# Layer 0's index stage and both stick-breaking stages in a new order: which instruction goes ahead of which on five engines

## What is computed

```python
# stick-breaking branch, per head and block of 128 queries
z = q @ k.T * dh ** -0.5
log_1m = where(mask, log_sigmoid(-z), 0)
csum = cumsum(log_1m)
a = where(mask, exp(log_sigmoid(z) + csum[-1:] - csum), 0)
y_a = a @ v
# sparse branch: scores that choose 128 keys for each query
s_idx = relu(einsum('bqhd,bkd->bqhk', iq, ixk) * IDX_DIM ** -0.5)
score = einsum('bqh,bqhk->bqk', iw * IDX_HEADS ** -0.5, s_idx)
_, sel = top_k(score, topk)
# latent branch
k_b = rope(rms_norm(concat(k_nope, k_pe)), cos, sin)
```

## Time and profile before

| | us |
|---|---|
| median of 3 runs (1336.82 to 1338.01) | 1337.74 |
| the profiled execution's own time | 1335.52 |
| its span in the trace | 1333.8 |
| PE busy | 1268.9 (95%) |
| DVE busy | 773.2 (58%) |
| ACT busy | 609.0 (46%) |

### The profile page before, as it was taken

One profiled execution on the slowest core, in us unless ns is written; L12 is line 12 of the kernel. 1 busy time (PEld: TensorE's weight loads), 2 busy tenths in 40 slices (PEclk: granted clock), 3 DMA queues, 4 the chain that ended last, 5 costly groups with the idle time before them and its releaser, 6 DMA issues.

```text
span 1333.8 us, 17870 instructions
## 1 busy us (share of the span) xinstructions
PE 1268.9 (95%) x6530; PEld 959.7 (72%) x6538; DVE 773.2 (58%) x1572; ACT 609.0 (46%) x1131; POOL 194.4 (15%) x316
## 2 busy tenths in 40 slices
PE   5898999999899999999999999999999999999998
PEld 5556666555578888888888876655556888888887
DVE  5878777888634344434456477878864424434442
ACT  4346566666653232233244365676666322323330
POOL 1372111133420000000000021113343000000000
PEclk9999999999999999999999999999999999999999
DMA  7244012201322333333332312220123322333321
GB/s 219 86 137 100 31 61 48 63 1 40 91 93 95 95 95 108 104 97 103 92 84 78 96 32 64 48 64 1 34 78 112 96 95 64 125 95 95 95 95 63
DMA packets 118568, 109.15 MB, mean 82 GB/s; under 512 B 34512, under 2 KB 101200, under 8 KB 118480
## 3 DMA queue, kind: packets, MB, share of 16 engines
q1 hardware_dynamic: 118480, 107.99, 27.1%
HBM read 100.64 MB, written 7.34 MB: 81 GB/s over the span
## 4 chain that ended last, share of the span: by engine, by line
PE 76%; DVE 9%; ACT 8%; issue 5%; SPq 1%; DMA 1%; POOL 0%; ACTq 0%; DVEq 0%
PE bank L837 20%; PE bank L839 20%; PE bank L838 20%; PE bank L983 3%; PE bank L1151 2%; PE bank L1194 2%; PE bank L1178 2%; PE bank L792 1%; DVE w_lo L729 1%; PE bank L1007 1%; ACT w_hi L723 1%; DVE probs L2043 1%; ACT soft L1482 1%; PE bank L1024 1%; ACT soft L1484 1%
## 5 line engine op out<-in xcount | busy, mean ns | idle before, releaser
L837 PE MATMUL bank<-h_hi,w_hi 128*128 128x512 f32 (+1 forms) x928 | 361.5, 390 | 4.0 <-DVE w_lo L729 2.2
L839 PE MATMUL bank<-h_hi,w_lo 128*128 128x512 f32 (+1 forms) x928 | 353.5, 381 | 0.0
L838 PE MATMUL bank<-h_lo,w_hi 128*128 128x512 f32 (+1 forms) x928 | 353.2, 381 | 0.0
L729 DVE TENSOR_TENSOR w_lo<-raw,w_hi 128x2048 fp32r<-128x2048 f32 (+2 forms) x98 | 189.1, 1931 | 119.4 <-ACT w_hi L723 119.3
L837 PEld LDWEIGHTS bank<-h_hi,w_hi 128*128 128x128 f32 x928 | 176.4, 190 | 50.5 <-issue 12.1
L723 ACT CAST w_hi<-raw 128x2048 fp32r<-128x2048 f32 (+2 forms) x100 | 159.1, 1593 | 112.5 <-PE bank L839 110.1
L839 PEld LDWEIGHTS bank<-h_hi,w_lo 128*128 128x128 f32 x928 | 176.2, 190 | 33.4
L838 PEld LDWEIGHTS bank<-h_lo,w_hi 128*128 128x128 f32 x928 | 176.4, 190 | 32.7 <-issue 1.9
L1666 ACT ACTIVATE gate<-bank,gains 128x512 f32<-128x512 f32 x48 | 33.0, 688 | 166.1 <-PE bank L839 166.1
L2228 POOL TENSOR_SCALAR probs<-probs,stat 128x128 f32<-128x128 f32 (+3 forms) x128 | 76.0, 594 | 147.3 <-DVE stat L1998 139.9
L837 PE MATMUL bank<-br_hi,w_hi 128*128 128x512 f32 x192 | 74.7, 389 | 0.0
(11 more groups left out here) (239 smaller groups left out, 2228.1 us busy)
## 6 DMA issues: line engine op xcount, KB each, us to landing
raw<-in_w_in SPq DMA_DIRECT2D x56, 1024.0 KB, 5.2
raw<-in_w_branch SPq DMA_DIRECT2D x12, 1024.0 KB, 5.2
raw<-in_w_out SPq DMA_DIRECT2D x8, 1024.0 KB, 5.0
bias<-bias_dram SPq DMA_DIRECT2D x16, 256.0 KB, 3.1
bias<-bias_dram SPq DMA_DIRECT2D x16, 192.0 KB, 2.6
x_sb<-in_x SPq DMA_DIRECT2D x4, 512.0 KB, 4.5
bias_dram<-bias_out SPq DMA_DIRECT2D x8, 256.0 KB, 2.9
raw<-in_w_in SPq DMA_DIRECT2D x4, 512.0 KB, 4.6
```

The costliest lines, as they stand in the source:

```text
L729: e.tensor_tensor(w_lo[:, s % RING, a:b], raw[:, s % RAW, a:b], w_hi[:, s % RING, a:b].bitcast(F32), ALU.subtract).then_inc(*lo_signal(nam ...
L837: pe.matmul(out_ap, lh, rh, start=start and i == 0, stop=False)
L838: pe.matmul(out_ap, lh, rl, start=False, stop=False)
L839: mm = pe.matmul(out_ap, ll, rh, start=False, stop=stop and i == n - 1)
```

## The change

Seven edits in the order of the code; nothing is computed otherwise, and no instruction is added but for a pair that is issued one by one.

1. DVE: the comparisons of G 3 go ahead of the three small ix_k operations, and those of G 7 ahead of the remainder of slab 2.
2. ACT and DVE: slab 5 is rounded ahead of the first index relu, not behind the fourth; its remainder is taken ahead of score 0, not score 4.
3. ACT: the sine goes between relu 15 and 16, the second table load between relu 19 and 20; both stood ahead of the copies of sa_v.
4. DVE: `first_rope` is split in two, ahead of scores 16 and 20.
5. ACT and POOL, both layers: for i mod 4 = 1 `stick_probs(i - 1)` and its masks go ahead of `softplus(i)` and its masks.
6. ACT, both layers: for i mod 4 = 2 `stick_probs(i - 1)` and `rounded(i)` alternate by head. In step 15 the norm of ds_q2 goes ahead of `softplus(15)`.
7. PE, both layers: `prep_q(0)` goes ahead of `pv_of(14)`.

```diff
@@ PE
+                    if i == STEPS:
+                        prep_q(0)
                     if i >= 2:
                         pv_of(i - 2)
                     if NORM_AT.get(i) in EARLY:
                         norm_tile(NORM_AT[i])
                     fill(i, "a")
-                    if i == STEPS:
-                        prep_q(0)
@@ ACT, index stage
+                    hi(5)
                     index_relus(0)
-                    hi(5)
                     index_relus(1)
                     index_relus(2)
                     index_relus(3)
+                    e.wait_ge(*angle_step.at("angle"))
+                    e.activation(ang[64:P, :], turns[64:P, :], ACT.Sin).then_inc(*cos_done.tick("sin"))
                     index_relus(4)
+                    e.preload_act_table_set("natural_log_exp_and_others")
                     index_relus(5)
...
-                if layer.l == 0:
-                    e.wait_ge(*angle_step.at("angle"))
-                    e.activation(ang[64:P, :], turns[64:P, :], ACT.Sin).then_inc(*cos_done.tick("sin"))
-                    e.preload_act_table_set("natural_log_exp_and_others")
@@ ACT, stick-breaking
+                    if i % ST == 1:
+                        stick_probs(i - 1)
+                    if i == STEPS - 1:
+                        norm_scale(NORM_AT[i])
                     softplus(i)
                     split_part(i, 0)
-                    early = i % 2 == 0 and i % ST
+                    early = i % ST == 2
                     if early:
-                        rounded(i)
+                        for head in range(2):
+                            stick_probs(i - 1, head)
+                            rounded(i, head)
                     tile_done(DONE.get((i, "a")))
-                    if NORM_AT.get(i) in EARLY:
+                    if NORM_AT.get(i) in EARLY and i < STEPS - 1:
                         norm_scale(NORM_AT[i])
-                    if i:
+                    if i and i % ST in (0, 3):
                         stick_probs(i - 1)
@@ DVE
+                if layer.l == 0:
+                    reaches(e, 3, 4)
                 e.tensor_copy(ix_k_low[top, :], dbank("k_pe")[top, :]).then_inc(*dve_evac.tick("ix_k hi"))
...
-                    reaches(e, 3, 7)
+                    reaches(e, 4, 7)
                     ix_q_parts(0)
+                    reaches(e, 7, 8)
                     split_lo(e, SLABS[2])
-                    reaches(e, 7, 11)
+                    reaches(e, 8, 11)
...
-                    if layer.l == 0 and u == 4:
+                    if layer.l == 0 and u == 0:
                         split_lo(e, SLABS[5])
+                    if layer.l == 0 and u == 16:
+                        first_rope_products()
+                    if layer.l == 0 and u == 20:
+                        first_rope_sums()
```

More of the change, by code:

```diff
@@ L1484, in softplus, with rounded @@
                         e.activation(v, v, ACT.Ln, bias=1.0).then_inc(*stick_exp.tick("ln", u))
-                def rounded(p):
+                def rounded(p, head=None):
                     for u, o, pair, kt, w in stick_units(p):
+                        if head not in (None, o):
+                            continue
                         e.wait_ge(*sp_masked.at(u))
@@ L1492, in rounded, with stick_probs @@
                         e.copy(sp_hi[:, o, SOFF[kt]:SOFF[kt] + w], soft[u % 4][:, 0:w]).then_inc(*sp_rounded.tick(u))
-                def stick_probs(p):
+                def stick_probs(p, head=None):
                     for u, o, pair, kt, w in stick_units(p):
+                        if head not in (None, o):
+                            continue
                         e.wait_ge(*stick_sum.at(u))
@@ L1767, in ix_q_parts, with first_rope_products, first_rope_sums @@
                                     ).then_inc(*dve_evac.tick(f"ix_q{j}"))
+                def first_rope_products():
+                    rows, low_rows = slice(64, 96), slice(96, P)
+                    e.wait_ge(*cos_done.at("sin"))
+                    e.wait_ge(*gains_in.at("b", DEPTH - 1, 2))
+                    e.tensor_scalar(cos_sin[64:P, :], ang[64:P, :], sign[64:P, :], None, ALU.mult).then_inc(*setup_dve.tick("cs"))
+                    e.wait_ge(*setup_dve.at("cs"))
+                    e.scalar_tensor_tensor(turns[rows, :], k_rope[low_rows, :], gain[low_rows, 4:5], cos_sin[low_rows, :],
+                                           ALU.mult, ALU.mult).then_inc(*dve_evac.tick("kr low"))
+                    e.scalar_tensor_tensor(k_rope[rows, :], k_rope[rows, :], gain[rows, 4:5], cos_sin[rows, :],
+                                           ALU.mult, ALU.mult).then_inc(*dve_evac.tick("kr0"))
+                def first_rope_sums():
+                    rows, low_rows = slice(64, 96), slice(96, P)
+                    e.wait_ge(*dve_evac.at("kr0"))
+                    e.tensor_tensor(k_rope[low_rows, :], k_rope[rows, :], turns[rows, :], ALU.add).then_inc(*dve_evac.tick("kr1"))
+                    e.tensor_tensor(k_rope[rows, :], k_rope[rows, :], turns[rows, :], ALU.add).then_inc(*dve_evac.tick("kr"))
                 e.wait_ge(*dense.at("k_pe"))
                 top, low = slice(0, IDX_DIM), slice(IDX_DIM, 2 * IDX_DIM)
+                if layer.l == 0:
+                    reaches(e, 3, 4)
                 e.tensor_copy(ix_k_low[top, :], dbank("k_pe")[top, :]).then_inc(*dve_evac.tick("ix_k hi"))
@@ L1936, in stick_out @@
                     e.tensor_copy(y[:, pair, :], bank[Y][:, :]).then_inc(*y_out["stick"].tick(pair))
[L1938 to L1947, removed]
-                                           ALU.mult, ALU.mult).then_inc(*dve_evac.tick("kr0"))
-                    e.wait_ge(*dve_evac.at("kr0"))
-                    e.tensor_tensor(k_rope[low_rows, :], k_rope[rows, :], turns[rows, :], ALU.add).then_inc(*dve_evac.tick("kr1"))
-                    e.tensor_tensor(k_rope[rows, :], k_rope[rows, :], turns[rows, :], ALU.add).then_inc(*dve_evac.tick("kr"))
-                if layer.l == 0:
-                    first_rope()
                 for i in range(STEPS):
@@ L2192, in _, with mask_probs @@
                                     channel_multiplier=1).then_inc(*score_masked.tick(t))
+                def mask_probs(p):
+                    for u, o, pair, kt, w in stick_units(p):
+                        d = stick_a[:, o, 0:P]
+                        e.wait_ge(*stick_prob.at(u))
+                        e.affine_select(out=d, in_=d, pattern=[[1, P]], compare_op=ALU.is_gt, fill=0.0, base=0,
+                                        channel_multiplier=-1).then_inc(*prob_masked.tick(u))
                 for i in range(STEPS + 1):
+                    if i % ST == 1:
+                        mask_probs(i - 1)
                     if i < STEPS:
@@ L2199, in _ @@
                                             channel_multiplier=-1).then_inc(*sp_masked.tick(u))
-                    if i:
-                        for u, o, pair, kt, w in stick_units(i - 1):
-                            d = stick_a[:, o, 0:P]
-                            e.wait_ge(*stick_prob.at(u))
-                            e.affine_select(out=d, in_=d, pattern=[[1, P]], compare_op=ALU.is_gt, fill=0.0, base=0,
-                                            channel_multiplier=-1).then_inc(*prob_masked.tick(u))
+                    if i and i % ST != 1:
+                        mask_probs(i - 1)
                     if i == 2:
```

## The result

The changed kernel took 1324.34 us in the median of 4 executions (1322.54 to 1326.56), the kernel before 1337.80 beside it: a ratio of 0.9902, 95% interval 0.9882 to 0.9921. That is 13.5 us faster, and 13.4 against the 1337.74 from which the prediction started; 1326.3 was predicted. The profiled execution took 1326.56, with a span of 1324.8, so it is the longest of the four, and 8.96 us under the profiled execution of before.

The account below looks back on a forecast made before the run. PE was busy 1268.9 of 1333.8 us, so only its waits could be saved, unless its clock moved. Terms 4.3 + 3.0 + 1.6 + 1.1 + 1.4 = 11.4 us off the 1337.74 median gave 1326.3, range 1322.3 to 1331.3.

Parts of the forecast that it names:

- Bias table, 4.3 us: Bias table, edit 1: PE through at 46.6 instead of 50.9, 4.3 us saved, clock included.
- Index scores, 3.0 us: Index stage, edits 2 to 4: of 4.4 us of waits for relu and sa_v, 1.4 paid back, 3.0 saved.
- With 2.3 score 0 is done at 100.0: Index scores: if slab 5's remainder takes 2.3 us on DVE, score 0 ends at 100.0 and relu 3 at 100.4.
- score 4 at 103.4: Index scores: score 4 at 103.4 gives relu 7 at 103.9, wanted at 104.3, so the 2.0 us wait goes.
- Clock at step 0, 1.6 us: Step 0 of layer 0: fills follow shorter pauses of 0.6 and 1.1 us and run at full clock, 1.6 us saved.
- Clock at ix_q0, 1.5 us: ix_q0 behind G 3: with a pause of 0.4 us the clock stays up, another 1.5 us saved.
- the first rival: Clock falls again behind new pauses, taking back 1.2 us at ix_q0 and 1.6 at step 0: 1329.1; chance 0.19.
- Stick-breaking, 1.1 and 1.4 us: Stick-breaking stages, edits 5 and 6: key sums first saves 1.1 us in layer 0 and 1.4 in layer 1.
- two of the rivals: Softplus held behind key sums: stick-breaking gains nothing, 1331, chance 0.12; or the kernel gets slower, 1341, chance 0.02.
- prep_q, 0 us: End of each stick-breaking stage, edits 6 and 7: prep_q(0) ahead of pv(14) saves 0 us, bounds -0.3 and +1.6 a layer.
- waits for its norm product: prep_q(0) overwrites the bank of ds_q2, so it waits for that norm product, 248.77 to 249.52 before the change.
- my two clock terms: Full clock kept at ix_q0, 1.5 us, and in the fills of step 0, 1.6 us; 3.1 us together.

Follow-up runs that it names:

- POOL waiting: Changed kernel in which POOL waits for score 3 before the angle's three products and sums; 1325.82 us, ratio 0.9921.
- bias table: The kernel before with edit 1 alone; 1331.90 against 1337.64 us, ratio 0.9955.
- sums first: The kernel before with edit 5 and the alternation of edit 6 alone, both layers; 1335.85 against 1337.64 us, ratio 0.9989.
- norm and prep_q: The kernel before with edit 7 and the norm of ds_q2 ahead of softplus(15) alone; 1338.61 against 1337.64 us, ratio 1.0010.
- the other seven: Changed kernel, its repeat, edits 2 to 4 alone, and changed kernel with norm product first, POOL's wait, steps 9/13 undone or edit 2 undone; ratios 0.9885 to 0.9971.
- rotated key later: Changed kernel with the rotated key's products and sums moved from the index scores to ahead of rest(4); 1321.68 us, ratio 0.9893.
- two edits: Changed kernel with ds_q2's norm product right behind clip(15) and the rotated key ahead of rest(4); 1319.97 us, ratio 0.9869.
- three edits: Changed kernel with ds_q2's norm product behind clip(15), the rotated key ahead of rest(4) and POOL's wait for score 3; 1318.81 us, ratio 0.9859.
- the repeated one: The changed kernel itself run once more with more executions, against the kernel before; 1324.41 us, ratio 0.9912.

## Why the prediction was right, and where it was not

The time fell inside the range, and 2.0 us under the forecast. That it fell so near is in part luck: in the profiled pair the index scores brought 1.5 us less than the term, step 0's clock 1.6 less and the latent stage took 2.0, while the two stick-breaking stages brought 2.5 more; the median then moved 4.4 us further than the profiled pair. Step by step:

- **Bias table, 4.3 us: right**, 4.5 measured, and 4.1 with the edit alone. The pauses came where I had put them, but smaller: 0.44 and 1.20 us. At G 10, where I had 1.5, no idle time is named, but the last eight matmuls of the group take 1.29 us in place of 0.61, so 0.7 us of the pause stands inside PE's busy time.
- **Index scores, 3.0 us: too high by half**, 1.5 measured. The term was also added up wrong: of 4.4 us, 0.6 at sa_v and 1.1 at slab 6 are paid back, 1.7 and not 1.4, which leaves 2.7. The failed step is "With 2.3 score 0 is done at 100.0" and the "score 4 at 103.4" behind it: the price of the scores beside POOL. The remainder did take 2.3 us. But POOL's sum had begun beside it, could not end, and then kept score 0 from ending, and POOL's next sums slowed scores 2 and 4. From the remainder's start to the end of score 4 I had 6.45 us; it took 8.14, 0.55 more for score 0 and 1.1 more for scores 1 to 4. So relu 7 starts late, and unit 11 waits the 0.96 us; I had kept 1 us for a slow remainder, at unit 7:

```profile
98.76 1.66 DVE L1869 SCALAR_TENSOR_TENSOR score<-ix_relu,ix_w,score 128x384 f32<-128x384 f32 x1
```
```profile
100.51 0.49 ACT L1380 ACTIVATE ix_relu<-bank 128x384 f32<-128x384 f32 x1 [1.19 <-DVE score L1869]
```

The contention fell on the instructions behind the one that I priced. The Trainium skill (SBUF — State Buffer, Who interferes with whom) calls the port pair an exclusive lock, taken by whoever comes first for its whole instruction; the 3.21 us of POOL's sum, and the 1.07 us of the scores with POOL waiting, agree. At sa_v 0.92 us stayed in place of 0.6, and the 0.77 at the remainder of slab 6 was less than the 1.1 that I had taken. The waits thus give 1.7 us, and PE's busy time from the bias table to z(1), 37.3 us against 37.0 before, takes 0.3 back.
- **Clock at step 0, 1.6 us: right in the mean, not in the profiled execution.** My term was a certainty; it is a chance. The count over 14 profiles says more than either trace, though its rows are small: at a chance of 4 in 7, 4 of 4 would come about one time in ten, and so would 0 of 3 (the last two rows). That the length of the wait matters is likely, and not shown.

| wait of PE right ahead of z(0) | kernels | profiles with half clock in step 0 |
|---|---|---|
| 2.4 us | before, bias table, sums first, norm and prep_q | 4 of 4 |
| 0.9 us, and 0.8 at the first fill | the other seven | 4 of 7 |
| 0, and 0 at the first fill | rotated key later, two edits | 0 of 2 |
| 0.4 us, and 0.8 at the first fill | three edits | 0 of 1 |

- **Clock at ix_q0, 1.5 us: right.** Each of the 10 profiles with edit 1 has full clock from 32 to 52 us; each of the 4 without it has a half-clock stretch there, two of them later than in the earlier trace rows, at ix_q1, and one at both. The three at ix_q1 follow the wait of 3.42 us at G 7, so what I held against the first rival, that no slow stretch came behind it, was one draw.
- **Stick-breaking, 1.1 and 1.4 us: too low**, 2.3 and 2.7 measured. Of z(6), pv(4) and z(7), I had 1.55 us less 0.2; here it is 2.0 less 0.2. DVE's chain was as I had it: clip(6) came at 167.46, which is 0.2 us earlier in the frame of before. ACT's was shorter:

```profile
169.99 0.37 ACT L1503 ACTIVATE stick_a<-bank 128x256 f32<-128x256 f32 x1
170.26 0.50 ACT L1493 CAST sp_hi<-soft 128x384 fp32r<-128x384 f32 x1
170.66 0.39 ACT L1503 ACTIVATE stick_a<-bank 128x256 f32<-128x256 f32 x1
```

From softplus's end to the second exponential's end it is 1.0 us, since successive instructions overlap by 0.1; I had 1.35. The larger miss is two waits that I left out: step 10 alternates too, and the 0.42 us at z(11) go with it; and the 0.3 at pv(8) go with edit 5 in step 9, since they are back where it is undone. The losses by step 9 were 0.44, not 0.25. The fear behind two of the rivals, that softplus behind the sums eats the gain, was unfounded: undoing it in steps 9 and 13 gains only 0.5 us a layer.
- **prep_q, 0 us: right for the changed kernel** (0.2), since "waits for its norm product" named the binding step: 1.37 us in place of 1.64. What I had not seen is what it prevents. Without it the alternation's gain ends in a longer wait at pv(14) and a half-clock stretch behind it, as the alternation alone shows. Counted with the alternation, it is worth 2.4 us in either layer.
- **The clock elsewhere.** No term of mine reached beyond step 0. The profiled execution lost 2.0 us between the stick-breaking stages, 1.7 of it in a half-clock stretch of the latent stage, behind a wait of 1.34 us that is in both kernels; the repeated one lost 0.4 there. The clock of all executions rose from 0.9943 to 0.9969, and 0.0026 of 1335 us is 3.5. That is near the 3.1 of my two clock terms, but the mean clock doesn't say in which place it was won, so it isn't shown to be the same 3.1. It does say why the median gained 13.4 us while the profiled pair shows 9.0: both profiled executions have 0.996, above the mean of the kernel before and below that of the changed one, and both lie 2.2 us off their medians. Which pauses cost how much clock in which execution stays open: a profile shows one draw each.

The Trainium skill (TensorE: Matmul & The Clock Gate, Part 1) says that the throttled level is the default and that the moment of the change varies between runs. The table agrees that it varies, 4 of 7 at equal waits; no run here gives a price for a single pause.

## What to carry to other kernels

Price a contention on both sides and for the instructions behind it: ask which instruction on the other engine is held, when it lets go, what starts just then, and what that engine issues next beside it. Where an edit removes waits of PE of 2 us and more ahead of small matmuls, count the clock behind them as a chance, and compare kernels by many executions with their mean clock, not by two profiles. And do not add up parts of a change: a part that gains nothing alone, such as prep_q ahead of pv(14), can be what lets the other's gain through.

## What was unexpected of the hardware

Half-clock stretches cost 1.5 to 1.7 us each and follow pauses as short as 0.9 to 1.3 us, in some executions and not in others. Five per thousand of clock, from 0.992 to 0.997, went with 5.9 us of time in the kernel before. And a POOL sum, which takes 1.29 us elsewhere, started 0.24 us into a DVE remainder of 2.30 us, ended 3.21 us after its start, and with POOL's next two instructions drew out three scores on DVE to 3.59 us from 1.07; without the held sum it was 3.08.
